# Query product in a PEER block: paired products of 512 columns, halves added on VectorE

## The reference

```python
def peer(h, w_pq, sub_key_1, sub_key_2, u_table, v_table):
    q = jnp.dot(h, w_pq).reshape(B, S, PEER_HEADS, 2, PEER_KEY_DIM // 2)
    s1 = jnp.einsum('bshe,ke->bshk', q[..., 0, :], sub_key_1)
    s2 = jnp.einsum('bshe,ke->bshk', q[..., 1, :], sub_key_2)
    v1, i1 = lax.top_k(s1, PEER_TOPK)
    v2, i2 = lax.top_k(s2, PEER_TOPK)
    cand = (v1[..., :, None] + v2[..., None, :]).reshape(..., PEER_TOPK * PEER_TOPK)
    vals, ci = lax.top_k(cand, PEER_TOPK)
    ...                      # idx from i1, i2, ci; g = softmax(vals)
    a = einsum('td,tkd->tk', ht, u_table[it]); w = gelu(a) * gt
    return einsum('tk,tkd->td', w, v_table[it])
```

## Time and profile before

| | |
|---|---|
| median of 3 runs | 3156.36 us (3153.74 to 3160.82) |
| profiled execution | 3157.6 us |
| its span, first to last instruction | 3156.0 us |
| TensorE busy | 3087.9 us, 98% |
| TensorE weight load | 2643.2 us, 84% |
| VectorE busy | 2254.4 us, 71% |
| ScalarE busy | 1438.4 us, 46% |
| GpSimd busy | 711.6 us, 23% |
| mean granted clock of TensorE | 0.992 |

### The profile page before, as it was taken

How to read it: one execution, slowest core, us unless ns; L and a number is a source line. 1 busy time by engine, 2 the same in 40 slices (tenths; PEclk the granted TensorE clock), 3 DMA queues, 4 the chain that set the end, 5 groups by cost and what they waited for, 6 DMA issues and landing times.

```text
span 3156.0 us, 43109 instructions
## 1 busy us (share of the span) xinstructions
PE 3087.9 (98%) x16124; PEld 2643.2 (84%) x16124; DVE 2254.4 (71%) x2683; ACT 1438.4 (46%) x1469; POOL 711.6 (23%) x513
## 2 busy tenths in 40 slices
PE   8999899999999988999989999999999999999998
PEld 6888788888888877888779888888888888888887
DVE  7766888888888878556688888766665555555556
ACT  5556544444444455446554443444444343434343
POOL 1100000000000000000002888888881101110110
PEclk9999999999999999999989999999999999999999
DMA  8444677777789865784435777888876766676763
GB/s 281 174 174 178 236 279 279 276 280 276 276 299 338 300 253 190 254 329 149 161 133 166 241 221 210 263 257 257 258 241 216 256 241 250 242 257 242 250 243 136
DMA packets 195361, 754.25 MB, mean 239 GB/s; under 512 B 53827, under 2 KB 53859, under 8 KB 124851
## 3 DMA queue, kind: packets, MB, share of 16 engines
q1 hardware_dynamic: 129988, 664.86, 58.4%
q0 software_dynamic: 55904, 70.92, 8.3%
q10 hardware_dynamic: 9360, 17.04, 1.5%
HBM read 714.82 MB, written 37.93 MB: 239 GB/s over the span
## 4 chain that ended last, share of the span: by engine, by line
PE 91%; DVE 4%; DMA 2%; ACT 1%; issue 1%; DVEq 0%; SPq 0%; ACTq 0%
PE bank L456 26%; PE bank L444 16%; PE bank L446 16%; PE bank L445 16%; PE bank L461 14%; DMA ring<-in_first 1%; DMA ring<-in_down 1%; PE bank L579 1%; DVE raw_lo L2168 0%; PE bank L926 0%; DVE misc L2332 0%; PE bank L450 0%; ACT ffn_hi L1533 0%; PE bank L567 0%; DVE raw_lo L2460 0%
## 5 line engine op out<-in xcount | busy, mean ns | idle before, releaser
L456 PE MATMUL bank<-h_both,ffn_hi 128*128 128x512 f32 x3440 | 820.6, 391 | 0.2 <-ACT ffn_hi L1719 0.2
L2915 DVE TENSOR_TENSOR part_lo<-ring,ffn_hi 128x2048 fp32r<-128x2048 f32 x254 | 582.3, 2293 | 324.2 <-ACT ffn_hi L2025 321.1
L2025 ACT ACTIVATE ffn_hi<-ring 128x2048 fp32r<-128x2048 f32 x250 | 479.2, 1917 | 611.9 <-PE bank L461 395.9
L456 PEld LDWEIGHTS bank<-h_both,ffn_hi 128*128 128x128 f32 x3440 | 633.1, 188 | 124.2 <-ACT ffn_hi L1719 0.6
L3273 POOL DMA_INDIRECT weight_dram<-misc x256 | 557.7, 2178 | 88.1 <-issue 75.7
L444 PE MATMUL bank<-ffn_hi,coef_hi 128*128 128x512 f32 x1008 | 392.1, 389 | 0.0
L445 PE MATMUL bank<-part_lo,coef_hi 128*128 128x512 f32 x1008 | 392.1, 389 | 0.0
L446 PE MATMUL bank<-ffn_hi,coef_lo 128*128 128x512 f32 x1008 | 392.1, 389 | 0.0
L2168 DVE TENSOR_TENSOR raw_lo<-ring,ffn_hi 128x2048 fp32r<-128x2048 f32 (+1 forms) x131 | 297.7, 2276 | 113.4 <-ACT ffn_hi L1533 112.4
L1533 ACT ACTIVATE ffn_hi<-ring 128x2048 fp32r<-128x2048 f32 x133 | 254.5, 1915 | 264.8 <-DMA ring<-in_first 99.8
L1719 ACT ACTIVATE ffn_hi<-ring 128x2048 fp32r<-128x2048 f32 x87 | 166.6, 1917 | 263.5 <-DMA ring<-in_gateup 261.4
(11 more groups left out here) (476 smaller groups left out, 4910.4 us busy)
## 6 DMA issues: line engine op xcount, KB each, us to landing
ring<-in_u_table SPq DMA_DIRECT2D x128, 1024.0 KB
ring<-in_v_table SPq DMA_DIRECT2D x128, 1024.0 KB
misc<-in_w_ada SPq DMA_DIRECT2D x192, 512.0 KB
ring<-in_gateup SPq DMA_DIRECT2D x88, 1024.0 KB
ring<-in_first SPq DMA_DIRECT2D x56, 1024.0 KB
ring<-in_down SPq DMA_DIRECT2D x44, 1024.0 KB
ring<-in_stream SPq DMA_DIRECT2D x40, 1024.0 KB
ring<-in_wo_pq SPq DMA_DIRECT2D x32, 1024.0 KB
```

The costliest lines, as they stand in the source:

```text
L456: nc.tensor.matmul(out[:, 0:2 * S], hi[:, k * P:(k + 1) * P], x_pair(k), start=k == 0, stop=False)
L2025: a.activation(part_hi[j % PARTS], raw[j % RAW], ACT.Copy).then_inc(sem("hi_ready"), 1)
L2915: v.tensor_tensor(part_lo[j % PARTS], raw[j % RAW], part_hi[j % PARTS].bitcast(F32), ALU.subtract).then_inc(sem("lo_ready"), 1)
```

## The change

The products of a query chunk take the form of the expert stage. High weights multiply high and low input side by side in one product of 512 columns; low weights multiply the high input into columns 256 to 511. Chunk 0 does it slice by slice (`paired_products`), the other 15 chunks do all high products first (`high_pass`), then wait for the low part, then the low ones (`low_pass`). The query is then the sum of the bank's two halves. VectorE forms it (`tensor_reduce`) where ScalarE copied it, so the copy goes from ScalarE's order, and a sum goes into VectorE's order ahead of each low part. The sums of the last four chunks stand ahead of low parts of expert chunks; that of chunk 15 stands alone ahead of the second choice.

```diff
                 for j in range(8):
                     n = SPLIT_PQ + j + 8 * it
-                    if n == SPLIT_PQ + 1:
-                        pe.wait_ge(sem("hi_ready"), n + 1)
-                        wait_bank(pe, "pq", j, it, 8)
+                    pe.wait_ge(sem("lo_ready" if n == SPLIT_PQ else "hi_ready"), n + 1)
+                    wait_bank(pe, "pq", j, it, 8)
+                    if n == SPLIT_PQ:
                         for k in range(KD):
-                            high_products(out_bank("pq", j)[:, 0:S], ffn_hi[n % PARTS][:, k * P:(k + 1) * P],
-                                          h2_hi[:, k, :], h2_lo[:, k, :], k == 0)
-                        wait_lo(pe, n)
-                    else:
-                        wait_lo(pe, n)
-                        wait_bank(pe, "pq", j, it, 8)
-                    for k in range(KD):
-                        if n == SPLIT_PQ + 1:
-                            m = nc.tensor.matmul(out_bank("pq", j)[:, 0:S], raw_lo[n % RAW][:, k * P:(k + 1) * P],
-                                                 h2_hi[:, k, :], start=False, stop=k == KD - 1)
-                            continue
-                        ks = slice(k * P, (k + 1) * P)
-                        if n == SPLIT_PQ:
+                            ks = slice(k * P, (k + 1) * P)
                             pe.wait_ge(sem("x_lo_out"), TURN_AT["h2"] + k + 1)
                             if k + 4 < KD:
                                 h2_turn(k + 4)
-                        m = split_products(out_bank("pq", j)[:, 0:S], ffn_hi[n % PARTS][:, ks], raw_lo[n % RAW][:, ks],
-                                           h2_hi[:, k, :], h2_lo[:, k, :], k == 0, k == KD - 1)
+                            m = paired_products(out_bank("pq", j), ffn_hi[n % PARTS][:, ks], raw_lo[n % RAW][:, ks],
+                                                h2_hi[:, k, :], h2_pair(k), k == 0, k == KD - 1)
+                    else:
+                        high_pass(out_bank("pq", j), ffn_hi[n % PARTS], h2_pair)
+                        wait_lo(pe, n)
+                        m = low_pass(out_bank("pq", j), raw_lo[n % RAW], h2_hi)
                     m.then_inc(multiplied, 1)
...
-            def query(j, it):
-                wait_multiplied(a, "pq", j, it, 8)
-
-                if j >= 2:
-                    a.wait_ge(sem("scores"), it * 8 + j - 1)
-                a.activation(qb[:, j % 2, :], out_bank("pq", j)[:, 0:S], ACT.Copy).then_inc(taken, 1)
...
                 for j in range(8):
-                    query(j, it)
                     if j:
                         score_copy(j - 1, it)
                     upper_in(SPLIT_PQ + PARTS + j + 8 * it)
...
+            def query(j):
+                wait_multiplied(v, "pq", j)
+                if j >= 2:
+                    v.wait_ge(sem("scores"), j - 1)
+                v.tensor_reduce(qb[:, j % 2, :], halves(bank[out_no("pq", j) % 4]), AXX, ALU.add).then_inc(taken, 1)
+
+            def query_lower(j):
+                query(j)
+                lower_in(SPLIT_PQ + PARTS + j)
+
             for j in range(4):
-                lower_in(SPLIT_PQ + PARTS + j)
+                query_lower(j)
                 ranks(j)
-            lower_in(SPLIT_PQ + 8)
+            query_lower(4)
...
             for j in range(2):
-                lower_in(SPLIT_PQ + 14 + j)
+                query_lower(10 + j)
                 ranks(4 + j)
             for j in range(2):
+                query(12 + j)
                 lower(j)
                 ranks(6 + j)
+            query(14)
             lower(2)
+            query(15)
             choose(1, 0)
```

More of the change, by code:

```diff
@@ L3021, in _ @@
             best(0, 0)
-            lower_in(SPLIT_PQ + 9)
+            query_lower(5)
             best(0, 1)
@@ L3025, in _ @@
             best(1, 0)
-            lower_in(SPLIT_PQ + 10)
+            query_lower(6)
             best(1, 1)
@@ L3029, in _ @@
             rows_cols()
-            lower_in(SPLIT_PQ + 11)
+            query_lower(7)
             hot(0, 0)
@@ L3033, in _ @@
             address(0, 0)
-            lower_in(SPLIT_PQ + 12)
+            query_lower(8)
             weights(0)
             hot(1, 0)
-            lower_in(SPLIT_PQ + 13)
+            query_lower(9)
             hot(1, 1)
```

## The result

| | before | after |
|---|---|---|
| median of 4 runs | 3156.89 us (3153.74 to 3160.82) | 3184.42 us (3181.95 to 3186.08) |
| profiled execution, its span | 3157.6, 3156.0 | 3184.0, 3182.4 |
| mean granted clock of TensorE | 0.992 | 0.988 |

The ratio is 1.0088 [1.0076, 1.01]: the change makes the kernel 27.5 us slower. Predicted were 3181.0 (3170 to 3189). The time lies 3.4 above the forecast, so inside the range, but 0.4 above the likeliest case's own band (3178 to 3184).

A forecast was written before the change was run, and what follows sets the result against it. TensorE bounds the kernel, the query stage passing one for one to the end. A stage 19.8 us longer through VectorE's sums and waits, plus 4.8 for two clock falls, makes 24.6: median 3156.4 to 3181.0, range 3170 to 3189.

The forecast's parts named there:

- likeliest case: Whole kernel: the forecast itself, median within 3 us of 3181, own band 3178 to 3184; chance 0.50.
- more than forecast: Rival, whole kernel: third clock fall, sums of 0.75 us and slower pace after the stage give 3186; chance 0.14.
- a third fall of the clock: TensorE before the last key scores: an idle of about 2.4 us could slow the clock again, 2.4 us more.
- The gain of the pairing: TensorE, query stage: chunks take 5.57 not 5.76 us; fifteen chunks gain 2.9 us if TensorE stays the bound.
- The sums: VectorE, query stage: 16 sums of two bank halves at 0.65 us each add 10.4 us.
- The walk through the order: Query stage, step by step: VectorE and TensorE wait for each other, so the stage ends 19.8 us later.
- the sums beyond what TensorE could hide: Query stage: VectorE's added work accounts for about 7 of the 19.8 us, three waits for the rest.
- The clock: TensorE after idles of 5.5 and 6.5 us: two falls of 2.4 us each, together 4.8, bounds 0 and 8.
- Full clock: Rival: TensorE's clock doesn't fall after the idles, so 3156.4 + 19.8 = 3176; chance 0.22, shared with one fall.
- Work alone: Rival, query stage: only VectorE's work counts, waits don't grow; +14 us, 3170; chance 0.09.
- TensorE as the bound: Rival, query stage: TensorE stays the bound and the kernel gets faster, 3153; chance 0.03.
- My condition: For the faster rival: VectorE's step with its sum under 6.01 us, needing sums under 0.15 us against 0.61.

The follow-up runs named there:

- E1: The kernel before with paired products, ScalarE still copying only the bank's first half (two of three products left out of the query); 3154.94 us, ratio 0.9997.
- E5: The changed kernel with 5, 17, 20 and 5 spare products on TensorE ahead of key scores 6, 7, 9 and 15; 3178.15 us, ratio 1.007.
- E6: The changed kernel's products, sums and rankings in another order, each sum near its chunk's end, rankings cut and pushed back; 3153.42 us, ratio 0.9989.
- E8: The changed kernel with key scores 7 behind chunk 8 and the first choice's exponential ahead of high part 12; 3170.15 us, ratio 1.0039.
- E7: The changed kernel with key scores 7 and their score copies moved behind chunk 8; 3180.12 us, ratio 1.0072.
- E4: The changed kernel with each query sum made twice, one after the other, on VectorE; 3191.75 us, ratio 1.0111.
- E2: The changed kernel with the old three products of 256 columns and a plain VectorE copy in place of the sum; 3183.15 us, ratio 1.0081.
- E3: The changed kernel with ScalarE's first exponential two high parts earlier, ahead of that of chunk 12; 3179.52 us, ratio 1.0076.

## Why the prediction was right

**The bound.** TensorE in the query stage, one for one to the end: confirmed, 26.1 us in the stage and 26.4 in the span. The range held, but the likeliest case's band (3178 to 3184) was missed by 0.4: the median is 1.6 from the 3186 of "more than forecast" and 3.4 from the forecast, and one of the three things that rival named, a third fall of the clock, did come.

**The gain of the pairing.** 2.9 forecast, 2.6 in E1. On TensorE itself it is there; it can't be seen in the result, because VectorE sets the pace.

**The sums.** 0.69 us on the engine, 0.61 to the next start; I took 0.65 for the step. A ranking step takes 1651.34 - 1644.85 = 6.49 us, forecast 6.54.

**The walk through the order.** It is the heart of the prediction, and each of its waits is in the trace:

| | forecast | after |
|---|---|---|
| TensorE idle before key scores 6 | 2.5 | 2.89 |
| TensorE idle before key scores 7 | 5.5 | 5.19 |
| VectorE waits for high part 12 | 4.4 (+2.4 by the clock) | 6.17 |
| VectorE waits for the exponential | 5.1 | 4.75 |
| VectorE waits for high part 15 | 0.3 (+2.4 by the clock) | 3.31 |
| TensorE idle before key scores 9 | 6.5 | 6.46 |
| stage longer, clock aside | 19.8 | 20.2 (E5) |

The idle before most other key scores is shown as 0.2 us and not 0.5. The step is nevertheless as long as forecast: one with a stop of 0.22 takes 6.49, one without 6.03 (E1), so a stop costs 0.24 us beside its idle. 0.1 of it shows in the key scores themselves (0.71 behind a stop, 0.61 without). With it the stage adds up: idles 21.4 less 0.8 before, 20.6; two falls of 2.7 and 2.9, 5.6; ten more stops at 0.24, 2.4; pairing -2.6; together 26.0 against 26.1 measured.

**What of it is work, what order.** Here the text put it wrong. It called about 7 of the 19.8 us "the sums beyond what TensorE could hide". E6 has all the sums, and its stage is shorter than before. The work that doesn't fit in the stage needn't be in it: the rankings of chunks 6 and 7 can stand between expert blocks. E8, with both waits of the middle gone and the rest of the order kept, still loses 14.7 us against its before. So none of the 19.8 is work that has to be paid; the sums cost through the order, each ahead of work that others need, or behind work that no one does.

**The clock.** Two falls of 2.4 us were forecast. Both came where forecast, right behind the idles of 5.19 and 6.46 us. They lasted about 5.4 and 5.8 us after the restart, so 2.7 and 2.9 us were lost. E5 gives 5.9 for both and what hangs on them; the forecast was 4.8. The third fall, behind the last key scores, was only in the rival case of more. It came too and cost 1.6. The stage's 26.1 in place of 24.6 and the 1.6 of the third fall make 27.7, where the medians show 27.5 and the forecast was 24.6. The term that was sized too small is the clock's: 5.9 and 1.6 against 4.8. Two falls had been read before, which cost 1.7 and 3.1 us, and their mean was forecast for each; the two here cost 2.7 and 2.9, and the loads and the exponential hang on them.

**The rivals.** Full clock (3176): E5 shows that it would have been 3178. Work alone (3170): needs the stop and the wait for the exponential away, and E8, which takes them away, lies at 3170.15. That the two agree so closely is luck: the rival still had 3.7 us of waiting for the exponential and no fall of the clock, E8 has no such wait, but falls and a late load. TensorE as the bound (3153): E6 is a kernel in which no sum is late, and it lies at 3153.4, a stage 3.2 shorter where that rival said 3.6. It took a new order. My condition, sums of under 0.15 us, was also taken wrong from its own rows: 6.01 less 5.89 is 0.12.

## What to carry to other kernels

Before an instruction moves to another engine, compare the step it lands in, not the engine's busy share: here 16 x 0.61 us cost 27 us in one order and nothing in another. In an order written by hand each instruction has a time at which its input is ready and one at which its output is needed; an instruction for the bounding engine belongs right at the first, and work that no one awaits behind the second. A circle over a ring buffer (engine waits for result, load waits for engine, result waits for load) turns one late result into several waits.

## What was new in the hardware's behaviour

- **Idles of two to three microseconds are a toss.** A fall followed idles of 2.09 (E7), 2.56 (after), 2.65 (E8), 2.67 (E7) and 2.81 us (E4, the last one), and none followed 1.79, 2.05 and 2.09 (both E4) and 2.82 us (E2). The same 2.09 us stand on both sides, so the length of the idle alone does not decide. In the query stage all idles from 3.78 us (E3) on brought one, except where spare products filled them. E2 after its last idle, and E4 after its first and a middle one (windows; the clock is the third number from the end):

```profile
1760.50:1767.00 6.50, 6.50 (x39) 5.75 (x39) 2.76 (x2) 2.60 (x3) 5.17 (x5) 1.00 1.06 411
```

```profile
1649.00:1655.00 6.00, 5.91 (x35) 5.25 (x36) 5.65 (x19) 2.30 (x2) 0.00 (x0) 1.00 0.36 153
1751.00:1759.00 8.00, 7.09 (x43) 6.13 (x43) 7.62 (x20) 2.60 (x3) 6.97 (x4) 1.00 0.48 120
```

- **Spare work can be a gain.** 47 products that no one needs made the changed kernel some 6 us faster: 27.5 us over its before without them, 21.9 with them (E5), 5.9 in the stage.
- **Single loads come late.** In E3 and E8 one of the loads took 6.3 and 6.6 us from issue to use, where the others of the stage's end take 4.7 to 5.9. VectorE waited 1.60 and 1.95 us for them, ahead of the last sum. GpSimd's scatters (L3270) were running then, but they ran beside the punctual loads too. Whether they delay single ones was not tested.
